# A six-layer transformer stack on one Trainium2 core: three layers' modulation vectors computed by VectorE instead of TensorE

## The reference, cut to what matters

```
cond = silu(c)                                    # 1024 values
for i in range(4):
    mod = cond @ w_mod[i] + b_mod[i]              # w_mod[i]: 1024 x 3072
    shift, scale, gate = split(mod, 3)
    h = rms_norm(x, norm_pre_g[i]) * (1 + scale) + shift
    o = mixer_i(h)                                # gla, sgu, fox, gla
    x = x + gate * rms_norm(o, norm_post_g[i])
```

## Time and profile before

| | |
|---|---|
| device time, three runs | 3170.28, 3186.34, 3186.37 us, median 3186.34 us |
| span of the profiled execution, first to last instruction | 3174.8 us |
| busy: PE, DVE, ACT, POOL | 2981.2, 1669.9, 1192.7, 307.2 us |
| mean granted TensorE clock | 0.971 of full speed |

### The profile page before, as it was taken

The page is one execution under the profiler, slowest core; times in us unless marked ns, Lnnn a source line. Parts: engine busy times, 40 slices in busy tenths (PEclk is TensorE's granted clock), DMA queues, the critical chain, the costliest instruction groups (busy, mean ns, idle before and its releaser), DMA issues.

```text
span 3174.8 us, 54076 instructions
## 1 busy us (share of the span) xinstructions
PE 2981.2 (94%) x22916; PEld 2420.0 (76%) x22916; DVE 1669.9 (53%) x2947; ACT 1192.7 (38%) x2156; POOL 307.2 (10%) x449
## 2 busy tenths in 40 slices
PE   7999999999999999978888999999999998999998
PEld 4767887756877688768866788888887876788887
DVE  3245445435442656767656653555566636654444
ACT  4314435446441455433344452111114435642121
POOL 1010020000001000043330010101110100000000
PEclk9999999999999999988889999999999999999999
DMA  6284222280224622000010023333341350033221
GB/s 228 80 304 144 80 88 81 83 298 19 95 79 157 234 102 70 22 24 24 23 68 27 1 73 80 126 126 111 116 153 67 92 96 25 8 100 106 98 101 66
DMA packets 172586, 307.59 MB, mean 97 GB/s; under 512 B 22694, under 2 KB 44007, under 8 KB 172089
## 3 DMA queue, kind: packets, MB, share of 16 engines
q1 hardware_dynamic: 134448, 253.35, 23.7%
q0 software_dynamic: 12048, 40.24, 4.1%
q10 hardware_dynamic: 25849, 10.56, 1.2%
HBM read 295.95 MB, written 6.81 MB: 95 GB/s over the span
## 4 chain that ended last, share of the span: by engine, by line
PE 75%; DVE 14%; ACT 6%; DMA 2%; issue 2%; POOL 1%; ACTq 0%; DVEq 0%; SPq 0%; POOLq 0%
PE psum L419 19%; PE psum L421 19%; PE psum L420 19%; PE psum L962 3%; PE psum L577 2%; PE psum L981 2%; DVE small L1126 2%; PE psum L2509 2%; DVE weights_r L363 2%; DVE arena L873 1%; PE psum L2499 1%; PE psum L996 1%; DVE x_lat L876 1%; ACT feat L686 1%; ACT weights_r L354 1%
## 5 line engine op out<-in xcount | busy, mean ns | idle before, releaser
L363 DVE TENSOR_TENSOR weights_r<-weights,weights_r 128x2048 fp32r<-128x2048 f32 (+1 forms) x161 | 360.0, 2259 | 387.6 <-ACT weights_r L354 387.6
L419 PE MATMUL psum<-feat_r,weights_r 128*128 128x512 f32 (+1 forms) x1536 | 539.1, 351 | 2.2 <-DVE weights_r L363 1.2
L420 PE MATMUL psum<-feat_r,weights_r 128*128 128x512 f32 (+1 forms) x1536 | 536.5, 349 | 0.0
L354 ACT ACTIVATE weights_r<-weights 128x2048 fp32r<-128x2048 f32 (+1 forms) x161 | 302.1, 1896 | 623.0 <-DMA weights<-in_w_ffn_gate 220.1
L421 PE MATMUL psum<-feat_r,weights_r 128*128 128x512 f32 (+1 forms) x1536 | 535.8, 349 | 0.0
L419 PE MATMUL psum<-weights_r,feat_r 128*128 128x512 f32 (+2 forms) x1344 | 522.3, 389 | 12.1 <-DVE feat_r L718 8.8
L421 PE MATMUL psum<-weights_r,feat_r 128*128 128x512 f32 (+2 forms) x1344 | 517.4, 385 | 0.0
L420 PE MATMUL psum<-weights_r,feat_r 128*128 128x512 f32 (+2 forms) x1344 | 516.9, 385 | 0.0
L419 PEld LDWEIGHTS psum<-feat_r,weights_r 128*128 128x128 f32 x1536 | 293.3, 191 | 45.8 <-issue 5.5
L420 PEld LDWEIGHTS psum<-feat_r,weights_r 128*128 128x128 f32 x1536 | 293.3, 191 | 36.4
L421 PEld LDWEIGHTS psum<-feat_r,weights_r 128*128 128x128 f32 x1536 | 292.7, 191 | 37.1
(11 more groups left out here) (510 smaller groups left out, 4199.2 us busy)
## 6 DMA issues: line engine op xcount, KB each, us to landing
weights<-in_w_mod SPq DMA_DIRECT2D x36, 2048.0 KB, 14.3
weights<-in_gla_w_in SPq DMA_DIRECT2D x24, 1024.0 KB, 7.3
arena<-in_w_mod_turned POOLq DMA_DIRECT2D x96, 256.0 KB, 3.0
weights<-in_w_ffn_gate SPq DMA_DIRECT2D x22, 1024.0 KB, 7.4
weights<-in_w_ffn_up SPq DMA_DIRECT2D x22, 1024.0 KB, 5.2
weights<-in_w_ffn_down SPq DMA_DIRECT2D x20, 1024.0 KB, 6.7
weights<-in_fox_w_in SPq DMA_DIRECT2D x16, 1024.0 KB, 7.1
weights<-in_sgu_w_in SPq DMA_DIRECT2D x12, 1024.0 KB, 6.3
```

The source lines that it names most:

```text
L354: act.e.activation(WEI_r[:, s * SLOT + HALF:s * SLOT + HALF + n], WEI_t[:, s * SLOT:s * SLOT + n], ACT.Copy).then_inc(*A.put(("weights", c ...
L363: dve.e.tensor_tensor(WEI_r[:, s * SLOT:s * SLOT + n], WEI_t[:, s * SLOT:s * SLOT + n], WEI_r[:, s * SLOT + HALF:s * SLOT + HALF + n].bitc ...
L419: pe.e.matmul(ps, lh, rh, start=first, stop=False)
L420: pe.e.matmul(ps, lh, rl, start=False, stop=False)
```

## The change

`SIDES` keeps only the modulations of layers one and five: nine entries instead of 18. Layer one's recurrence carries four (points 0, 2, 4, 6, the last fold at 7), layer four's three (points 0, 2, 4, fold at 5), layer three's attention none.

The modulations of layers two to four are computed by VectorE. `w_mod_turned` is the host's transposed copy of these weights. `SUMMED` has 72 steps, each one output column group of 128: `sp_summed` loads 128 rows x 1024 (512 KB) into one of two places, and `dve_summed` multiplies with the condition row and sums along it in one instruction. The load of step n waits for the instruction of step n-2. Loads are issued by SyncE behind named weight chunks, so later weight DMAs stand behind them in SyncE's stream. The condition row is written to memory by ScalarE's queue at the start, and broadcast to 128 partitions before step 0 and again before step 16, at the end of layer one. The steps of VectorE stand between its other work: 16 in layer one, 6 in its end, 18 in layer two, 28 in layer three (one behind each of the 16 q and k tiles, one behind each of the four v copies, one behind each of the eight z tiles), 4 in its end. `dve_summed_bias` adds the bias.

Because the sides are gone from layer three's attention, the take at its last projection chunk (n0 = 2560) now splits the first z chunk.

`att_on_act` no longer looks at masks: in narrow attentions VectorE copies the even units' turned exponentials and ScalarE the odd ones.

```diff
-SIDES = [(mod, n0) for mod in range(5) for n0 in range(0, (3 if mod < 4 else 6) * D, 2 * NMAX)]
-SIDES_BEGIN, SIDES_GLA, SIDES_SGU, SIDES_FOX = 2, {0: 6, 3: 5}, 0, 5
+SIDES = [(mod, n0) for mod in (0, 4) for n0 in range(0, (3 if mod < 4 else 6) * D, 2 * NMAX)]
+SIDES_BEGIN, SIDES_GLA, SIDES_SGU, SIDES_FOX = 2, {0: 4, 3: 3}, 0, 0
+
+SUMMED = [(mod, m) for mod in (1, 2, 3) for m in range(3 * KT)]
+SUMMED_GLA = 2 * KT
...
                 sp.e.dma_start(raw, src[:, q0:q0 + q, :]).then_inc(*w_in[s].put(("weights", c, j)))
+            for n in range(summed_behind.get((name, index, n0), 0)):
+                sp_summed(sp)
...
+    COND_ROW = FL_plain[:, 0:4, 512:768]
+    SUMMED_W = [grid(FEAT_t[:, 0:FEATS], KT)[:, 4 * h:4 * h + 4, 512:768] for h in range(2)]
+    summed_behind = {
+        ("gla_w_in", 0, 1536): 2, ("gla_w_in", 0, 0): 2, ("gla_w_in", 0, 512): 4, ("gla_w_in", 0, 2048): 2,
+        ("gla_w_in", 0, 2560): 4, ("w_mod", 0, 2048): 2, ("gla_w_out", 0, 512): 8,
+        ("sgu_w_in", 0, 1536): 3, ("sgu_w_in", 0, 0): 3, ("sgu_w_in", 0, 512): 1, ("sgu_w_in", 0, 2048): 3,
+        ("sgu_w_in", 0, 2560): 4, ("sgu_w_out", 0, 0): 4,
+        ("fox_w_in", 0, 512): 4, ("fox_w_in", 0, 1024): 4, ("fox_w_in", 0, 1536): 4, ("fox_w_in", 0, 2048): 4,
+        ("fox_w_in", 0, 2560): 2, ("fox_w_in", 0, 3072): 2, ("fox_w_in", 0, 3584): 4, ("fox_w_out", 0, 0): 4,
+        ("fox_w_out", 0, 512): 2}
...
+    def sp_summed(sp):
+
+        n = summed["sp"]
+        summed["sp"] = n + 1
+        mod, m = SUMMED[n]
+        if n == 0:
+            sp_cond_row(sp, "gla")
+        if n == SUMMED_GLA:
+            sp.wait_ge(*B.of((("end", 0), "turned")))
+            sp_cond_row(sp, "after")
+        if n >= 2:
+            sp.wait_ge(*V.of(("summed", n - 2)))
+        sp.e.dma_start(SUMMED_W[n % 2], io["w_mod_turned"][mod - 1, m * P:(m + 1) * P, :].rearrange(
+            "p (k c) -> p k c", k=4)).then_inc(*first_mod_in[n % 2].put(("summed", n)))
+
+    def dve_summed(dve, count=1):
+
+        for n in range(summed["dve"], summed["dve"] + count):
+            mod, m = SUMMED[n]
+            w = SUMMED_W[n % 2]
+            dve.wait_ge(*first_cond_in.of("gla" if n < SUMMED_GLA else "after"))
+            dve.wait_ge(*first_mod_in[n % 2].of(("summed", n)))
+            dve.e.scalar_tensor_tensor(w, w, 1.0, COND_ROW, ALU.mult, ALU.mult,
+                                       accum_out=MODC[:, mod * 24 + m:mod * 24 + m + 1]).then_inc(*V.put(("summed", n)))
+        summed["dve"] += count
...
         dve_take(dve)
+        if tag in (("end", 0), ("end", 2)):
+            dve_summed(dve, 4)
...
                 dve.e.tensor_copy(Y[:, t, 0:NMAX], K.at[at]).then_inc(*V.put(K.frees(V, at), (tag, "y", 0, t)))
+                if tag == ("end", 0) and pair[0] == tiles[0]:
+                    dve_summed(dve)
...
     def att_on_act(units, n):
         if att_narrow(units):
-            return bool(units[n]["bias"] or units[n].get("mask")) or n % 2 == 1
+            return n % 2 == 1
         return n % 2 == 1 and units[n]["nk"] > 256
...
                 dve_head_scale(dve, f_qn[r], K.at[at], f_ss, 8, FDH, A.of((T, "root", n0, t)),
                                [K.frees(V, at), (T, "qn", n0, t)])
                 calls += 1
+                dve_summed(dve)
...
                 dve.e.tensor_tensor(o, o, grid(f_zs[t % 2], 4), ALU.mult).then_inc(*V.put((T, "gated", n0, t)))
+                dve_summed(dve)
```

More of the change, by code:

```diff
@@ L191, in program @@
     keys_in = signal("window_values_in", 16)
+    first_cond_in, first_mod_in = signal("first_cond_rows", 16), [signal(f"first_mod_rows_{h}", 16) for h in range(2)]
     rpb_in, rpb_out, x_out = signal("rpb_in", 16), signal("rpb_out", 16), signal("x_out", 16)
@@ L197, in program @@
     cond_out, cond_in, mod_in = signal("cond_out", 16), signal("cond_rows_in", 16), [signal(f"mod_weights_{h}", 16) for h in range(2)]
-    every = [B, A, V, G, *w_in, cond_out, cond_in, *mod_in, const_in, x_in, ctx_in, *par_in, layer_in, bias_in, keys_in, down_in, rpb_in, rpb_out, x_out,
+    every = [B, A, V, G, *w_in, cond_out, cond_in, *mod_in, first_cond_in, *first_mod_in, const_in, x_in, ctx_in, *par_in, layer_in, bias_in, keys_in, down_in, rpb_in, rpb_out, x_out,
              *spill_out, sums_out, *decay_in, narrow_in, turns_in, *gate_out, *gate_in]
@@ L318, in program @@
     plan, chunks, held = slots_of(weight_plan())
-    taken, sided, folded = {}, {}, {}
+    taken, sided, folded, summed = {}, {}, {}, {}
     def weights_of(c):
@@ new lines, in sp_cond_row @@
+    def sp_cond_row(sp, name):
+        sp.wait_ge(*cond_out.of("first cond"))
+        sp.e.dma_start(COND_ROW, cond_dram[2].rearrange("m p -> (m p)").partition_broadcast(P)).then_inc(
+            *first_cond_in.put(name))
+    def sp_summed(sp):
[11 more added lines that the diff above has]
+            "p (k c) -> p k c", k=4)).then_inc(*first_mod_in[n % 2].put(("summed", n)))
@@ L522, in act_begin, with dve_summed_bias @@
+    def dve_summed_bias(dve, mod, m, n):
+        cols = MODC[:, mod * 24 + m:mod * 24 + m + n]
+        dve.chain()
+        dve.e.tensor_tensor(cols, cols, pcol("b_mod", mod * 24 + m, n), ALU.add).then_inc(*V.put())
     def act_begin(act):
@@ L534, in act_begin @@
         act.e.activation(cond2[:, :, 1], pcol("c_ctx_2", 0, 8), ACT.Silu).then_inc(*A.put("cond"))
+        act.chain()
+        act.e.dma_start(cond_dram[2].rearrange("m p -> p m"), cond1[:, :, 0],
+                        allow_slow_non_contiguous=True).then_inc(*cond_out.put("first cond"))
     def pe_begin(pe):
@@ L1352, in dve_gla @@
         T = ("gla", i)
+        sums = 1 if i == 0 else 0
         for n0 in (0, 512):
@@ L1358, in dve_gla @@
                 dve.e.tensor_copy(g_v[:, t, n0:n0 + NMAX], K.at[at]).then_inc(*V.put(K.frees(V, at)))
+                if n0:
+                    dve_summed(dve, sums)
             if n0 == 0:
@@ L1371, in dve_gla @@
         dve_take(dve)
+        dve_summed(dve, 2 * sums)
         dve.wait_ge(*A.of((T, "ln")))
@@ L1381, in dve_gla @@
                     dve.e.tensor_copy(g_k[:, m - 4, :], K.at[at]).then_inc(*V.put(K.frees(V, at)))
+                    if m < 6:
+                        dve_summed(dve, sums)
         V.mark((T, "qk"))
@@ L1384, in dve_gla @@
             dve_take(dve)
+            dve_summed(dve, 4 * sums)
+        if i == 0:
+            dve_summed_bias(dve, 1, 0, 2 * KT)
         V.mark((T, "in"))
@@ L1538, in dve_sgu @@
                 dve.e.bn_stats(s_st[:, t, 6 * h:6 * h + 6], s_v[:, t, n0:n0 + NMAX]).then_inc(*V.put())
+                if t:
+                    dve_summed(dve)
         for t in LAT:
@@ L1564, in dve_sgu @@
             dve_take(dve)
+            dve_summed(dve, 4)
+        dve_summed_bias(dve, 1, 2 * KT, KT)
+        dve_summed_bias(dve, 2, 0, 2 * KT)
         dve_side(dve, False)
@@ L1785, in dve_fox @@
                 dve.e.tensor_tensor(o, o, grid(f_zs[t % 2], 4), ALU.mult).then_inc(*V.put((T, "gated", n0, t)))
+                dve_summed(dve)
+            if n0 == 0:
+                dve_summed_bias(dve, 2, 2 * KT, KT)
+                dve_summed_bias(dve, 3, 0, 2 * KT)
     def first_y(i):
@@ L1819, in dve_first_end @@
         y, name, Y, off = first_y(i)
+        if i == 3:
+            dve_summed_bias(dve, 3, 2 * KT, KT)
         dve_to_feat(dve, T, LAT, before={(0, t - 1): lambda t=t: dve_sgu_mix(dve, t) for t in (2, 3)} if i == 1 else None)
@@ L3720, in run @@
         turns.clear()
-        for count in (taken, sided, folded):
-            count.update(pe=0, act=0, dve=0)
+        for count in (taken, sided, folded, summed):
+            count.update(pe=0, act=0, dve=0, sp=0)
         main(Lane(e, own))
@@ L3840 @@
     arrays, io = {}, {}
-    turned = {"w_mod_2_turned": _np.asarray(inputs["w_mod_2"])[1].T}
+    turned = {"w_mod_2_turned": _np.asarray(inputs["w_mod_2"])[1].T,
+              "w_mod_turned": _np.asarray(inputs["w_mod"])[1:].transpose(0, 2, 1)}
     for name, a in list(inputs.items()) + list(turned.items()) + list(constants().items()):
```

2 lines of the change are left out of this document (1 added, 1 removed).

## The result

The changed kernel takes 3214.2 us (median of four runs, 3210.8 to 3221.5) against 3185.6 before: ratio 1.0096, 95% interval 1.0068 to 1.0124. By the medians it is 28.7 us slower; 3191 was forecast, at most 3214. The ratios here leave out three disturbed executions (3739 and 4672 us of the kernel before, 7312 us of `best_window`).

A forecast was written before the change was run, and what follows sets the result against it. TensorE was taken as the limit over most of the kernel, with savings read from what ends last at each place. The terms summed to +5.0 us on the median of 3186.3, giving 3191 us, range 3158 to 3214.

The forecast's parts named there:

- Layer three's projections: Loads in SyncE's stream delay the weight chunks' DMAs, so TensorE stops 8.4, 3.8 and 3.8 us; with a later start, +17.2.
- Layer one's recurrence: Two sides fewer and a shorter tail, against a 6.0 us stop at the moved split and 3 for the clock: -2.7 us.
- layer four's: Layer four's recurrence: two sides removed, against a moved split of 5.8 us and 2 for the clock: -0.8 us.
- layer three's attention: Four sides and the one ahead of all go, less 3 us for the clock and -0.5 for copies: -19.7 us.
- the copies: VectorE copying even units in layer three's attention: ScalarE relieved, VectorE nearly full; booked -0.5 to +3 us, taken as -0.5.
- One step of the new work: A VectorE step takes 1.3 us, all 72 make 94; hidden in waits in layers one and two, 0.5 us for layer two.
- the end of layer one: Steps wait for loads of 3.8 us, the sum of squares comes 8.9 later, 3.5 are free: about +5.5 us.
- the end of layer three: Late output chunk and four following steps exceed the slack by 0.7 us, plus one step before the turn: +2 us.
- Rival A: Faster: the loads do not hold SyncE, stops shrink, the clock stays up and copies break even; 3161 us, chance 0.18.
- Rival B: Faster: TensorE's removed time comes out whole, -49 us plus the window attention's 3; 3140 us, chance 0.05.
- Rival C: Slower: low clock after six stops costs 3.4 us each, attention pairs lag; 3209 us, sign clock below 0.96, chance 0.19.
- Rival D: Slower: VectorE becomes the attentions' bound, 48 pairs at +0.3 us each; 3203 us, chance 0.12.

The follow-up runs named there:

- best_window: The changed kernel with loads reordered, condition row written later, sides moved, layer two's steps respread, none in the ends, ScalarE copying in the window attention: ratio 0.9925 to the kernel before.
- copies_alone: The kernel before with only the edit that gives even units' copies in the narrow attentions to VectorE: ratio 0.9995.
- writes_32b: The changed kernel with condition and gate writes meant as 32-byte pieces, which took effect for the gates only: end of layer one gives back 4.8 of 12.8 us.
- reordered: The changed kernel with only the 72 loads moved in SyncE's stream, behind the weight DMAs that can be issued first: span 3182.3 us.
- cond_late: The changed kernel with the condition values' write issued after the first tile's scaling, about 44 us, instead of at 14.6: the start adds 0.4 us instead of 6.5.

## Why the prediction was wrong

**Right in mechanism.** Layer three's projections: +17.2 forecast, TensorE waiting at its turning for L936 (L997 now); 16.6 came (14.2 in the table, where 2.4 of the removed first side go off), all of it gone when SyncE's stream is reordered. The mechanism is the forecast's; that the sum is so close is luck. The first stop was right (8.1 for 8.4), the other two were 2.6 and 2.7 us and not 3.8 each, the 1.2 of a later start did not show, and 3.2 us of low clock behind the first two stops, which the forecast had not booked here, filled the gap.

Layer one's recurrence: -2.7, measured -2.1; layer four's: -0.8, measured -2.8. The stop of the first is the forecast's, but `copies_alone`, whose code there is the old one, has -1.9 and -1.7, so these two sizes tell little. **Right in size:** layer three's attention: -19.7, measured -23.0 with those 2.4; one step: 1.3, measured 1.32; the copies: about 0, and the window +3, measured +1.5 to 1.9.

**The step that failed** is the end of "One step of the new work": "In layers one and two they hide in its waits ... I give layer two 0.5." It cost 13.6 us. The mechanism was the one that the prediction worked out for layer three, and it was not carried to layer two. There four loads stand ahead of the output weights' DMA, which left 12.1 us late, four full steps stand behind the take, and then comes the mix. With the loads reordered the stretch adds 3.4, without loads 1.2. The prediction asked whether VectorE has time and not when SyncE gets to the DMA behind. The steps there are also longer than forecast, 2.3 us for 1.3: GpSimd multiplies beside them.

**A term that was missing** is the start: the prediction has none for the new 4 KB write. It cost 6.5. **Terms mis-sized:** the end of layer one (+5.5, measured 12.8), where loads were taken at 3.8 us and one took 9 behind the gates' write; about 5 us of the difference are that write (`writes_32b`), some 2 the clock after the stop; the end of layer three (+2, measured 8.4), which is mended without the loads (2.1) or without steps there (1.4).

**Chance.** The 3.2 us of layer one's projections are a fall of the granted clock (0.51 over 108 to 112 us) while TensorE was busy without a gap; `copies_alone`, with the old code there, has it too (+4.8). The shared stretch swung from -2.0 to +12.4. The carry of a sum from a single span to a median hid 9 us: in the span the forecast was +5 and 38.3 came.

Rival A failed on what it was doubted for: a fast load does not change the order. Rival B's whole saving did not come. Rival C has the nearest number, 3209, but not the cause. The clock was 0.960, and 0.957 to 0.963 in the four executions, on both sides of its sign of 0.96. Behind the stops of layer one's end, the mix and the projections it cost 2.2, 1.4, 1.8, 1.4 and 0 us where C takes 3.4 each; in `reordered`, with the mix's stop and the projections' gone, it is 0.966. By the rule of the Trainium skill that was weighed there ("TensorE: Matmul & The Clock Gate", section "Why this matters for your kernels"), idle gaps between bursts of matmuls bring the low clock back, so a stop should cost more than its length. The trace agrees for the stops of 12.4, 10.0 and 8.0 us; of the two of 2.5 us one cost 1.4 more and the other nothing. Rival D did not show.

## What to carry to other kernels

When small loads that wait for a consumer are put into a queue that also feeds the bound engine, write down for each entry when its wait ends and when the next entry is due, for every stage and not only the tightest: here the same work, differently ordered, was worth 27 us of 3213. A 512 KB load issued right behind 2 MB of weights took some 9 us to land, so where it is needed soon it should go ahead. The new 4 KB write had to be priced by its 1024 pieces and by what was in flight beside it, and not by its bytes. And a sum that comes out right is to be checked stop by stop: in layer three's projections a wrong length and a clock that nobody had booked cancelled.

## What the runs showed of the hardware

While a write to DRAM in 1024 pieces of 4 bytes is in flight, the core's other transfers nearly stop: 74 GB/s for 387 over 4 us at the start (`cond_late` gives the 387 back), and 1 GB/s for 4 us in the end of layer one. As 128 pieces the write landed after 6.3 us, not 13.3.

VectorE's step on two SBUF operands took 2.3 us, not 1.22, while GpSimd multiplied two SBUF operands; GpSimd's product was longer too, 1991 ns on average for 1511 before. GpSimd's timeline, then VectorE's:

```profile
445.27 7.19 POOL L1547 TENSOR_TENSOR arena<-arena 128x512 f32<-128x512 f32 x4 [96.32 <-ACT arena L1600]
```
```profile
445.51 2.33 DVE L566 SCALAR_TENSOR_TENSOR feat<-feat 128x1024 f32<-128x1024 f32 x1
...
447.77 2.30 DVE L566 SCALAR_TENSOR_TENSOR feat<-feat 128x1024 f32<-128x1024 f32 x1
...
454.81 1.22 DVE L566 SCALAR_TENSOR_TENSOR feat<-feat 128x1024 f32<-128x1024 f32 x1 [1.26 <-DMA feat<-in_w_mod_turned]
```

The Trainium skill ("Advanced Engine Details and Errata", section "Miscellaneous Facts") says that GpSimd shares a read and a write interface with VectorE, in conflict where a VectorE instruction has two SBUF inputs; the rows agree and give the price.
